# A two-layer hybrid block on one core: another order of TensorE in each step of the mixer, with what moves along with it

## The chip, the cores and the metric

The kernel runs on one core of a Trainium2 chip. The metric is device time in microseconds from start to end of one execution. TensorE does the matrix products (PE in the profile, PEld its weight loads), VectorE is DVE, ScalarE is ACT, GpSimd is POOL, and SyncE (SP) issues the transfers.

## The reference, cut to what matters

```python
for l in range(2):                      # x is 512 x 1024, float32
    h = rmsnorm(x, norm_mix[l])
    ua, cq, ckv, kr, qc, kc, vc, ud = split(h @ w_in[l])     # 15 column chunks of 128
    ya = conformer_conv(ua, ...)        # gate, 31-tap causal convolution, layernorm, silu, @ conv_pw
    yb = mla(cq, ckv, kr, ...)          # 4 heads, causal softmax attention over 512 keys
    yc = diff_attention(qc, kc, vc, positions, rel_bias, ...)   # 4 heads, 2 softmax maps each:
                                        # p = a0 - lam * a1, then rmsnorm of the result
    yd = multiscale_pool(ud, pool_w, pool_scale)   # windows of 2, 4, 8, 16 tokens
    x = x + concat(ya, yb, yc, yd) @ w_out[l]
    x = x + memory_cross_attention(rmsnorm(x), mem, ...)     # K and V from 256 memory tokens
    x = x + conv_glu_ffn(rmsnorm(x), ...)
return rmsnorm(x, norm_final)
```

## The kernel before

Activations lie transposed: 128 features per partition tile, 512 tokens in a row. A weight matrix is streamed in chunks of 128 output columns (1024x128 floats). Each chunk n goes through the same four stations, with two buffers per station (b = n % 2): SP loads it to `raw`, ACT rounds it to `wh` (`hi`, L695), an engine subtracts to get the rest `wl` (`lo` on DVE at L937, or `lower` on POOL at L650), and TensorE's `gemm` (L1247 to L1249) does 8 tiles of three products, wh x hi, wh x lo and wl x hi. The result in PSUM bank `G[n % 2]` is taken over by DVE (`scaled`, L962) or ACT (L845). `hi(n)` waits for the end of gemm n-2, and `gemm(n)` for `wl` of n.

In each layer 11 chunks of `w_in` come first, then the small products of the latents, and then the mixer: a loop over 38 steps t (`for t in range(STEPS)`, written out in Python for each engine, so the order on each queue is fixed). Steps 0 to 15 take one tile each of the MLA attention (one head, 128 queries, 512 keys), steps 16 to 31 one tile of differential attention with two maps. For a tile:

- TensorE computes the scores into `SC` (L1353, or two products at L1362), at the head of its step.
- DVE adds mask or bias, negates and takes the minimum (`negatives`, L1035). ACT does exp with the row sum (`exp_map`, L754).
- One step later DVE takes the reciprocal of the sum (L1054, L1060); for two maps it also makes a weight (L1062) and adds the second map to the first (L1064). POOL multiplies the tile by the reciprocal (L673).
- `TURN_LAG` = 3 steps later TensorE transposes the tile (`turn`, L1322) and ACT copies it to `ptr` (`evict_pt`, L769), after the `exp_map` of its own step.
- Every second step TensorE multiplies two transposed tiles with the values (`weighted_pair`, L1333); it waits for both copies. Pair n is at step 2n+5.

In the same steps lie one chunk gemm or none (`CHUNK_AT`: chunks 11 to 14 of `w_in` at steps 0 to 3, chunks 15 to 22 of the memory's keys at steps 5 to 12, chunks 23 to 30 of its values at 16, 18, 20, 22, 24, 27, 30, 33), the convolution's 62 taps on DVE (`convolve`), and small products that share the two PSUM banks `V`: transposed values `vc` (step 4), pooling `pool0/1` (8, 12), layernorm sums `ln_mean` (10) and `ln_var` (14), `pw0/1` of the convolution (22, 26), memory values `vx0..3` (20, 24, 28, 36), `sub0/1` for the norm of the differential result (29, 37). `V_USES` lists the uses of those banks in order, with the engine that frees each. At steps 34 to 37 the first two chunks of `w_out` begin.

In PE's step before the change: scores, turn, small products, weighted pair, chunk.

Of the kernel before, what the change touches and what calls it, by code (L numbers as in the profile page):

```python
# [27 lines left out]
P = 128  # L28
# [41 lines left out]
for _name, _w in (("ident", P), ("ones", P), ("bones", P), ("pair", P), ("invf", 1), ("phase", 1),  # L70
# [12 lines left out]
V_USES = ([("stat_mix", "dve"), ("stat_q", "dve"), ("stat_kv", "dve"), ("kr", "act"), ("uq0", "dve"),  # L83
           ("uq1", "dve"), ("uq2", "dve"), ("uq3", "dve")] + [(f"kn{h}", "act") for h in range(4)] +
          [("vm0", "act"), ("vm1", "act"), ("vc0", "act"), ("vc1", "act"), ("pool0", "dve"), ("ln_mean", "dve"),
           ("mla0", "dve"), ("pool1", "dve"), ("ln_var", "dve"), ("mla1", "dve"), ("vx0", "act"), ("pw0", "dve"),
           ("vx1", "act"), ("pw1", "dve"), ("diff0", "act"), ("vx2", "act"), ("sub0", "dve"), ("diff1", "act"),
           ("vx3", "act"), ("sub1", "dve"), ("stat_xa", "dve")] +
          [(f"xo{i}", "dve") for i in range(8)] + [("stat_ffn", "dve")])

Y_ORDER = {6: "pool0", 2: "mla0", 7: "pool1", 3: "mla1", 0: "pw0", 1: "pw1", 4: "diff0", 5: "diff1"}
# [12 lines left out]
V_FREED = {owner: [n for n, o in V_USES if o == owner] for owner in ("dve", "act")}  # L104

# [5 lines left out]
CHUNK_AT = {**{t: 11 + t for t in range(4)}, **{t: 10 + t for t in range(5, 13)},  # L111
            **{t: N_WV + i for i, t in enumerate((16, 18, 20, 22, 24, 27, 30, 33))}}

POOL_LO = {15: 25, 17: 26, 19: 27, 21: 28, 23: 29, 26: 30}
TURN_LAG = 3
STEPS = 38


def tile_at(u):

    return 2 * (u // 8) + u % 2, u // 2 % 4, u % 2

# [21 lines left out]
def block_program(nc, xT, memT, pos, const, vecs, small, w_first, w_main, w_up, w_down, w_last, out):  # L144
    with ExitStack() as ctx:
# [65 lines left out]
        memh, _ = sb("memh", [P, KT, M], F32R, a_at)  # L211
        meml, _ = sb("meml", [P, KT, M], F32R, a_at + 8192)
# [4 lines left out]
        psa, _ = sb("psa", [P, 528], F32, a_at + 24576)  # L217
        psb, _ = sb("psb", [P, 528], F32, a_at + 24576 + 2112)
# [62 lines left out]
        m_hi, m_lo = sem("mem_hi"), sem("mem_lo")  # L281
# [246 lines left out]
        with nc.Fori(0, L) as layer:  # L528
            with nc.Block() as block:
# [17 lines left out]
                def _(sp):  # L547
# [12 lines left out]
                    loads_of(2, 2, w_main, src_base=2)  # L560
                    sp.dma_start(sw[:], small[layer]).then_inc(sw_in, 16)
                    sp.dma_start(memf[:], mem_norm).then_inc(memf_in, 16)
                    loads_of(4, 12, w_main, src_base=4)
                    loads_of(16, 10, w_main, src_base=16)
# [14 lines left out]
                    for n in range(26, 35):  # L579
                        load(n, n % 2, w_main[layer, n])  # L580
                        if n == 26:
                            for u in (2, 3, 0, 1):
                                load_bias(u)
                        elif n < 31:
                            load_bias(2 * n - 50)
                            load_bias(2 * n - 49)
                        elif n == 31:
                            for u in (12, 13, 14):
                                load_bias(u)
                        elif n == 32:  # L590
                            load_bias(15)
# [15 lines left out]
                def _(pool):  # L607
# [6 lines left out]
                    def window_sums(i):  # L614

                        if i == 0:
                            pool.wait_ge(g_full, N_WK)
                        pool.wait_ge(g_dve, 14 + i)
# [47 lines left out]
                    for u in range(32):  # L666
                        if u < 16:
                            pool.wait_ge(rec_in, u + 1)
                            e, m = ering[:, u % RING, :], u
                        else:  # L670
                            pool.wait_ge(p_ready, u - 16 + 1)
                            e, m = dring[:, 2 * u % 8, :], 2 * u - 16
                        pool.tensor_scalar(e, e, rec[:, m:m + 1], None, ALU.mult).then_inc(scaled_in, 1)  # L673
                        if u in (3, 5):
                            window_sums(u // 2 - 1)
                        if u in (4, 6):
                            window_differences(u // 2 - 2)
                        if u in POOL_LO:
                            lower(POOL_LO[u])
# [8 lines left out]
                def _(act):  # L688
# [13 lines left out]
                    def v_freed(name):  # L702

                        act.wait_ge(v_dve, V_FREED["dve"].index(name) + 1)

# [20 lines left out]
                    for n in range(3, 11):  # L726
# [45 lines left out]
                    for t in range(STEPS):  # L772
# [7 lines left out]
                        if t == 4:  # L780
                            act.wait_ge(memf_in, 16)
                            act.wait_ge(g_full, N_WK)
                            for k in range(KT):
                                act.activation(memh[:, k, :], memf[:, k, :], ACT.Copy,
                                               scale=v("g_mem", k)).then_inc(m_hi, 1)
                            for i in range(2):
                                act.activation(vc[:, :, P * i:P * i + P],
                                               v_wait(f"vc{i}").rearrange("p (t f) -> p t f", t=4),
                                               ACT.Copy).then_inc(v_act, 1)
                        if t == 6:  # L790
                            act.wait_ge(lam_in, 2)
                            act.activation(lam[:, 2:4], lam[:, 0:2], ACT.Exp).then_inc(lam_e, 1)
# [3 lines left out]
                        if t in (8, 12):  # L796
                            i = t // 4 - 2
                            act.activation(b_hi[:, 6 + i, :], v_wait(f"pool{i}"), ACT.Copy,
                                           scale=v("pscale", i)).then_inc(y_hi, 1)
                        if t == 12:  # L800
                            for i in range(2):
                                if i == 0:
                                    act.wait_ge(cent, 1)
                                else:
                                    v_freed("ln_mean")
                                act.activation(sqx[:, i, :], acc[:, i, :], ACT.Square).then_inc(cent_sq, 1)
                        if t == 14:
# [7 lines left out]
                        if t in (22, 26):  # L815
                            i = (t - 22) // 4
# [8 lines left out]
                        if t in (20, 24, 28, 36):  # L825
                            g = {20: 0, 24: 1, 28: 2, 36: 3}[t]
                            act.activation(vx[:, :, GW * g:GW * g + GW],
                                           v_wait(f"vx{g}").rearrange("p (m f) -> p m f", m=2), ACT.Copy).then_inc(v_act, 1)
                        if t in (29, 37):
                            i = t // 8 - 3  # L830
                            act.activation(rtmp[:], v_wait(f"sub{i}"), ACT.Sqrt, bias=c("eps5"),
                                           scale=1.0 / 64).then_inc(root, 1)
                        if t in (34, 37):
# [96 lines left out]
                def _(dve):  # L930
# [18 lines left out]
                    def inverse(name, roots, cols=slice(0, S)):  # L949
# [4 lines left out]
                        if cols.stop == S:  # L954
                            ins.then_inc(v_dve, 1)
                            own_v(name)

                    def scaled(n, dst, b=None):
# [10 lines left out]
                              cq[:, 0, :], cq[:, 1, :], ckv[:], qk[:, 0, :], qk[:, 1, :], qk[:, 2, :], qk[:, 3, :],  # L969
                              vct[:, 0, :], vct[:, 1, :], ud[:, 0, PPAD:], ud[:, 1, PPAD:]]  # L970
# [16 lines left out]
                    def latents(part):  # L987
# [7 lines left out]
                        else:  # L995
                            dve.wait_ge(root, 3)
                            dve.reciprocal(sqx[:, 0, :], sqx[:, 0, :]).then_inc(v_dve, 1)
                            own_v("stat_kv")
# [4 lines left out]
                    for n in range(11):  # L1003
# [21 lines left out]
                        if n >= 3:  # L1025
                            convolve({8: 0, 9: 1, 10: 4}.get(n, 3))
# [11 lines left out]
                    for t in range(STEPS + 1):  # L1038
# [12 lines left out]
                        if 1 <= t < 17:  # L1051
                            m = t - 1
                            dve.wait_ge(e_done, m + 1)
                            dve.reciprocal(rec[:, m:m + 1], sums[:, m:m + 1]).then_inc(rec_in, 1)  # L1054
                        elif 17 <= t < 33:

                            u, k = t - 17, 2 * t - 18
                            dve.wait_ge(e_done, k + 2)
                            e0, e1 = dring[:, 2 * u % 8, :], dring[:, (2 * u + 1) % 8, :]
# [5 lines left out]
                        if t < 4:  # L1065
                            convolve(4)
                        elif t > 4:
                            convolve(3)
                        if t == 4:
# [5 lines left out]
                        if t in (9, 13):  # L1075
                            i = t // 4 - 2
# [3 lines left out]
                        if t == 11:  # L1080
# [7 lines left out]
                        if t in (12, 20):  # L1088
# [8 lines left out]
                        if 15 <= t < 19:  # L1097
                            inverse("ln_var", 4, slice(P * (t - 15), P * (t - 14)))
                        if t == 18:
# [547 lines left out]
```

## Time and profile before

| | us |
|---|---|
| median of 3 runs | 1760.46 (1758.02 to 1761.1) |
| the profiled execution, its own time | 1760.47 |
| its span, first to last instruction | 1758.6 |
| PE busy in the span | 1630.3 (93%) |
| DVE, ACT, POOL busy | 1108.6, 698.8, 308.2 |
| mean granted TensorE clock | 0.962 of 2.4 GHz |

Busy shares are means over stages of different kind. The mixer of layer 0 lies at 197 to 393 us, that of layer 1 at 1019 to 1214 us; the large matrix products fill most of the rest. A number in brackets at the end of a row is the idle time of the engine just before it, with what ended it.

### The profile page before, as it was taken

To read this page: it belongs to the slowest core of one execution; us is meant where nothing else is said; L and a number is where in the kernel's file an instruction comes from. 1 tells how busy PE (TensorE), PEld (TensorE's weight loads), DVE (VectorE), ACT (ScalarE), POOL (GpSimd) and SP (SyncE) were. 2 spreads that over 40 slices of the span, in tenths; PEclk is the share of its full clock that TensorE was granted. 3 is DMA by queue.
4 is the path that set the end of the run, shared out by engine and by line. 5 is a ranking of instruction groups with operands and counts; after the bars stand their busy time and mean duration, and the time that the engine had idled before them with its cause. 6 is when DMAs were issued, how large, how long until landed. Compare 5 with 4: busy or idle time off the path is not lost. (4 is left out here: it accounts for less than half of the span.)

```text
span 1758.6 us, 21905 instructions
## 1 busy us (share of the span) xinstructions
PE 1630.3 (93%) x7472; PEld 1253.1 (71%) x7472; DVE 1108.6 (63%) x1592; ACT 698.8 (40%) x1074; POOL 308.2 (18%) x216
## 2 busy tenths in 40 slices
PE   6889979889999999999998988898999999999996
PEld 3567566568767888888876666666877788888874
DVE  8967785655345764764764867665444675575576
ACT  3132345753244432432442243764343442342343
POOL 6510174522002000000020027551101100000002
PEclk9989899999999999999998998999999999999998
DMA  3242122313202232323324212322211222322323
GB/s 134 52 148 84 49 72 96 102 51 100 84 24 84 96 95 96 97 96 96 95 82 138 75 48 61 109 97 72 91 54 60 84 96 96 96 95 96 96 84 107
DMA packets 46206, 153.38 MB, mean 87 GB/s; under 512 B 5808, under 2 KB 6064, under 8 KB 45232
## 3 DMA queue, kind: packets, MB, share of 16 engines
q1 hardware_dynamic: 46128, 152.34, 26.8%
q8 instruction: 49, 0.80, 0.2%
q14 instruction: 29, 0.24, 0.0%
HBM read 144.97 MB, written 7.34 MB: 87 GB/s over the span
## 5 line engine op out<-in xcount | busy, mean ns | idle before, releaser
L695 ACT ACTIVATE wh<-raw 128x1024 fp32r<-128x1024 f32 x246 | 260.4, 1059 | 660.9 <-PE psum L1249 660.9
L1247 PE MATMUL psum<-a_hi,wh 128*128 128x512 f32 x1072 | 426.1, 397 | 7.9 <-DVE wl L937 7.5
L1249 PE MATMUL psum<-a_hi,wl 128*128 128x512 f32 x1072 | 420.0, 392 | 0.0
L1248 PE MATMUL psum<-a_lo,wh 128*128 128x512 f32 x1072 | 420.0, 392 | 0.0
L937 DVE TENSOR_TENSOR wl<-raw,wh 128x1024 fp32r<-128x1024 f32 x234 | 288.6, 1234 | 193.4 <-ACT wh L695 193.2
L1247 PE MATMUL psum<-b_hi,wh 128*128 128x512 f32 x608 | 240.8, 396 | 10.6 <-DVE wl L937 6.1
L1247 PEld LDWEIGHTS psum<-a_hi,wh 128*128 128x128 f32 x1072 | 203.0, 189 | 57.6 <-DVE wl L937 11.5
L1248 PE MATMUL psum<-b_lo,wh 128*128 128x512 f32 x608 | 237.4, 390 | 0.0
L1249 PE MATMUL psum<-b_hi,wl 128*128 128x512 f32 x608 | 237.4, 390 | 0.0
L1248 PEld LDWEIGHTS psum<-a_lo,wh 128*128 128x128 f32 x1072 | 203.2, 190 | 44.9 <-issue 2.9
L1249 PEld LDWEIGHTS psum<-a_hi,wl 128*128 128x128 f32 x1072 | 202.9, 189 | 42.5
L1135 DVE TENSOR_TENSOR x_sb<-x_sb,psum 128x512 f32<-128x512 f32 (+1 forms) x80 | 54.8, 685 | 168.9 <-PE psum L1249 168.9
L1247 PEld LDWEIGHTS psum<-b_hi,wh 128*128 128x128 f32 x608 | 114.5, 188 | 40.3 <-DVE wl L937 9.5
L1248 PEld LDWEIGHTS psum<-b_lo,wh 128*128 128x128 f32 x608 | 114.5, 188 | 24.2 <-issue 1.0
L1249 PEld LDWEIGHTS psum<-b_hi,wl 128*128 128x128 f32 x608 | 114.5, 188 | 24.0
L660 POOL COPY ssum<-sqx 128x512 f32<-128x512 f32 x6 | 3.7, 610 | 725.8 <-ACT sqx L712 725.8
L962 DVE TENSOR_TENSOR up<-psum,rbc 128x512 f32<-128x512 f32 x88 | 60.9, 692 | 87.1 <-PE psum L1249 87.0
L673 POOL TENSOR_SCALAR ering<-ering,rec 128x512 f32<-128x512 f32 x32 | 56.6, 1774 | 281.8 <-DVE rec L1054 281.2
L981 DVE SCALAR_TENSOR_TENSOR acc<-conv_in,vec,acc 128x512 f32<-128x512 f32 x120 | 100.2, 835 | 2.8
L663 POOL TENSOR_TENSOR ssum<-ssum,sqx 128x512 f32<-128x512 f32 x42 | 68.4, 1628 | 140.6 <-ACT sqx L712 140.6
L472 DVE TENSOR_SCALAR ind<-posf,cst 128x512 fp32r<-128x512 f32 x128 | 83.8, 723 | 1.0 <-PE psum L509 0.9
L1247 PE MATMUL psum<-memh,wh 128*128 128x256 f32 x256 | 82.5, 322 | 0.0
(214 smaller groups left out, 2188.3 us busy)
## 6 DMA issues: line engine op xcount, KB each, us to landing
raw<-in_w_main SPq DMA_DIRECT2D x106, 512.0 KB, 3.5
raw<-in_w_up SPq DMA_DIRECT2D x88, 512.0 KB, 3.5
raw<-in_w_down SPq DMA_DIRECT2D x32, 512.0 KB, 3.5
raw<-in_w_last SPq DMA_DIRECT2D x16, 384.0 KB, 2.9
bias_scratch<-stage SPq DMA_DIRECT2D x64, 64.0 KB, 1.6
bias<-bias_scratch SPq DMA_DIRECT2D x16, 256.0 KB, 3.9
raw<-in_w_first SPq DMA_DIRECT2D x6, 512.0 KB, 3.5
sw<-in_small SPq DMA_DIRECT2D x2, 1152.0 KB, 6.9
```

What stands on the lines that cost most here:

```text
L472: dve.tensor_scalar(ind[:, g % 4, :], posf[:, 0:S], c("turn"), posf[:, bass.ds(S + s * 8 + g, 1)], ALU.mult, ALU.is_le).then_inc(ind_in, 1)
L660: pool.tensor_copy(ssum[:], sqx[:, 0, :]).then_inc(ss_in, 1)
L663: pool.tensor_tensor(ssum[:], ssum[:], sqx[:, k % 2, :], ALU.add).then_inc(ss_in, 1)
L673: pool.tensor_scalar(e, e, rec[:, m:m + 1], None, ALU.mult).then_inc(scaled_in, 1)
L695: act.activation(wh[:, b].rearrange("p k m -> p (k m)")[:, 0:width], raw[:, b, 0:width], ACT.Copy).then_inc(w_hi, 1)
L937: dve.tensor_tensor(wl[:, b].rearrange("p k m -> p (k m)"), raw[:, b, :], wh[:, b].rearrange("p k m -> p (k m)").bitcast(F32), ALU.subtrac ...
L962: dve.tensor_tensor(dst, G[b], rbc[:], ALU.mult).then_inc(g_dve, 1)
L981: ins = dve.scalar_tensor_tensor(acc[:, i, :], win, w, acc[:, i, :], ALU.mult, ALU.add)
L1135: dve.tensor_tensor(x_sb[:, at, :], x_sb[:, at, :], G[b].rearrange("p (o s) -> p o s", o=1), ALU.add).then_inc(g_dve, 1)
L1247: pe.matmul(out_ap, wh[:, b, k, :], his[:, k, :], start=(begin and i == 0), stop=False)
L1248: pe.matmul(out_ap, wh[:, b, k, :], los[:, k, :], start=False, stop=False)
L1249: last = pe.matmul(out_ap, wl[:, b, k, :], his[:, k, :], start=False, stop=(end and i == len(tiles) - 1))
```

## The change

The order of TensorE in a step becomes turn, small products, weighted pair, scores, chunk. Along with it:

- One more chunk of `w_in` (12 in all) comes ahead of the mixer, and the order of these is changed, so that the pooling input `ud` is early (`IN_ORDER`). Chunks 12 to 30 now lie at steps 0 to 7, then 9, 11, ... 23, then 26, 29, 32.
- POOL no longer multiplies by the reciprocals; DVE does, with one more tensor_scalar of 128x512 per tile (it replaces L1062 in the two-map tiles). POOL makes `wl` of all chunks 15 to 32 instead of six, and does the pooling windows ahead of the mixer.
- The memory operands `memh` and `meml` are laid out so that each tile can be written as soon as chunk 14 has used the tile of `a_hi` in its place (`a_used`).
- `pool0/1` go to steps 1 and 3, `vc` to 6 and 8, `ln_mean` to 11, `ln_var` to 15, `vx0..3` to 18, 22, 28, 36, `pw0/1` to 23 and 25, `sub0` to 30. Every fourth pair (n % 4 == 0) is one step later.
- A bank that holds a sum for a square root is free after ACT has read it (`root`), not after DVE's reciprocal.

```diff
-CHUNK_AT = {**{t: 11 + t for t in range(4)}, **{t: 10 + t for t in range(5, 13)},
-            **{t: N_WV + i for i, t in enumerate((16, 18, 20, 22, 24, 27, 30, 33))}}
-POOL_LO = {15: 25, 17: 26, 19: 27, 21: 28, 23: 29, 26: 30}
+IN_ORDER = [0, 1, 2, 3, 4, 5, 6, 13, 14, 7, 8, 9, 10, 11, 12]
+CHUNK_AT = {t: 12 + i for i, t in enumerate((0, 1, 2, 3, 4, 5, 6, 7, 9, 11, 13, 15, 17, 19, 21, 23, 26, 29, 32))}
+VX_AT = {18: 0, 22: 1, 28: 2, 36: 3}
+POOL_LO = range(N_WK, N_OUT + 2)
+def pair_step(n):
+    return 2 * n + 5 + int(n % 4 == 0)
...
@@ gpsimd
-                    for u in range(32):
-                        if u < 16:
-                            pool.wait_ge(rec_in, u + 1)
-                            e, m = ering[:, u % RING, :], u
-                        else:
-                            pool.wait_ge(p_ready, u - 16 + 1)
-                            e, m = dring[:, 2 * u % 8, :], 2 * u - 16
-                        pool.tensor_scalar(e, e, rec[:, m:m + 1], None, ALU.mult).then_inc(scaled_in, 1)
...
+                    for i in range(2):
+                        window_sums(i)
+                        window_differences(i)
+                    for n in POOL_LO:
+                        lower(n)
@@ scalar
-                        if t == 19:
+                        if t == 21:
+                            act.wait_ge(cn, 2)
                             for i in range(2):
-                                act.wait_ge(cn, i + 1)
                                 act.activation(sqx[:, i, :], sqx[:, i, :], ACT.Silu, ...)
@@ vector
+                            dve.wait_ge(rec_in, m + 1)
+                            dve.tensor_scalar(e, e, rec[:, m:m + 1], None, ALU.mult).then_inc(scaled_in, 1)
                         elif 17 <= t < 33:
...
-                            step(dve.scalar_tensor_tensor(wgt[:, u:u + 1], rec[:, k + 1:k + 2], lam[:, 4:5],
-                                                          sums[:, k:k + 1], ALU.mult, ALU.mult))
-                            dve.scalar_tensor_tensor(e0, e1, wgt[:, u:u + 1], e0, ALU.mult, ALU.add).then_inc(p_ready, 1)
+                            step(dve.tensor_scalar(e1, e1, rec[:, k + 1:k + 2], lam[:, 4:5], ALU.mult, ALU.mult))
+                            dve.scalar_tensor_tensor(e0, e0, rec[:, k:k + 1], e1, ALU.mult,
+                                                     ALU.add).then_inc(scaled_in, 1)
@@ tensor
                     for t in range(STEPS):
+                        if TURN_LAG <= t < 32 + TURN_LAG:
+                            turn(t - TURN_LAG)
+                        if t in (1, 3):
+                            i = t // 2
+                            pe.wait_ge(ud_done, 2 * i + 2)
+                            product(f"pool{i}", ...)
...
+                        if t in VX_AT:
+                            g = VX_AT[t]
+                            pe.wait_ge(g_act, 8 + 2 * g + 2)
...
+                        if t in PAIR_AT:
+                            weighted_pair(PAIR_AT[t])
                         if t < 16:
                             h, qb, _ = tile_at(t)
                             bank_seen(t)
```

## Rows read from the trace of the kernel before

**Rows 1.** The page, part 1: busy us, share of the span, instructions, by engine.

```profile
PE 1630.3 (93%) x7472; PEld 1253.1 (71%) x7472; DVE 1108.6 (63%) x1592; ACT 698.8 (40%) x1074; POOL 308.2 (18%) x216
```

**Rows 2.** Stages: length, busy of PE, PEld, DVE, ACT, POOL, clock, DMA share, GB/s.

```profile
197.00:293.00 96.00, 83.09 (x488) 64.21 (x486) 67.55 (x112) 43.14 (x83) 48.02 (x33) 0.93 0.23 76
293.00:393.00 100.00, 87.12 (x574) 60.83 (x569) 62.80 (x136) 64.52 (x129) 42.57 (x25) 0.93 0.23 76
1116.00:1214.00 98.00, 85.34 (x568) 59.42 (x566) 62.41 (x136) 64.12 (x129) 42.17 (x25) 0.95 0.22 76
700.00:800.00 100.00, 99.57 (x440) 82.08 (x439) 67.39 (x91) 39.47 (x49) 0.00 (x0) 1.00 0.31 96
```

**Rows 3.** PE's timeline: start, length, instruction, count; heads of steps 0, 1, 16, 17.

```profile
196.62 1.02 PE L1353 MATMUL psum<-km,qm 128*128 128x512 f32 x2
202.93 1.02 PE L1353 MATMUL psum<-km,qm 128*128 128x512 f32 x2
...
293.18 1.13 PE L1362 MATMUL psum<-qk 32*128 32x512 f32 x4
...
297.69 1.13 PE L1362 MATMUL psum<-qk 32*128 32x512 f32 x4
...
300.36 1.13 PE L1362 MATMUL psum<-qk 32*128 32x512 f32 x4
```

**Rows 4.** PE's timeline, layer 0: waits in steps 5, 10, 21, 33 and after 37.

```profile
231.20 1.98 PE L1333 MATMUL psum<-ptr,vm 128*64 128x128 f32 x16 [5.18 <-ACT vc L787]
...
262.33 0.66 PE L1322 MATMUL psum<-cst,ering 128*128 128x128 f32 x4 [2.96 <-POOL ering L673]
...
265.97 3.78 PE L1276 MATMUL psum<-acc,cst 128*128 128x512 f32 x4 [2.98 <-DVE acc L981]
...
317.65 1.09 PE L1333 MATMUL psum<-ptr,vc 128*64 128x128 f32 x16 [2.21 <-DVE b_lo L1091]
...
367.75 1.11 PE L1322 MATMUL psum<-cst,dring 128*128 128x128 f32 x4 [3.50 <-POOL dring L673]
...
393.07 0.50 PE L1247 MATMUL psum<-b_hi,wh 128*128 128x512 f32 x1 [1.78 <-DVE wl L937]
```

**Rows 5.** A stretch with a lowered clock, columns as in rows 2.

```profile
262.00:272.00 10.00, 6.69 (x22) 4.39 (x23) 3.84 (x7) 1.29 (x3) 4.25 (x3) 0.66 0.15 52
```

**Rows 6.** Timeline of DVE and ACT in step 17, after the scores at 297.69.

```profile
298.96 0.69 DVE L1035 CUSTOM_DVE_ANT_0 dring<-psum,bias 128x512 f32<-128x512 f32 x1 [2.28 <-PE psum L1362]
...
299.69 0.72 ACT L754 ACTIVATE dring<-dring,mins 128x512 f32<-128x512 f32 x1 [0.51 <-DVE mins L1035]
...
301.12 0.57 ACT L769 ACTIVATE ptr<-psum 128x512 f32<-128x512 f32 x1
```

**Rows 7.** ACT's timeline in step 19: the silu between its table loads.

```profile
310.16 1.28 ACT L813 ACT_TABLE_LOAD   x1
311.46 1.52 ACT L813 ACTIVATE sqx<-sqx,vec 128x512 f32<-128x512 f32 x2
...
317.15 1.06 ACT L695 ACTIVATE wh<-raw 128x1024 fp32r<-128x1024 f32 x1
318.10 0.39 ACT L845 ACTIVATE vxt<-psum 128x256 f32<-128x256 f32 x1
```

**Rows 8.** Timeline of POOL and DVE around 318 us.

```profile
318.29 2.35 POOL L650 TENSOR_TENSOR wl<-raw,wh 128x1024 fp32r<-128x1024 f32 x1 [3.78 <-ACT wh L695]
318.83 1.83 DVE L1062 SCALAR_TENSOR_TENSOR wgt<-rec,lam,sums 128x1 f32<-128x1 f32 x1
```

**Rows 9.** Groups of DVE by form, 196 to 400 us: count, busy us, mean ns, idle before.

```profile
L981 DVE SCALAR_TENSOR_TENSOR acc<-conv_in,vec,acc 128x512 f32<-128x512 f32 x33 | 29.9, 906 | 0.8
L937 DVE TENSOR_TENSOR wl<-raw,wh 128x1024 fp32r<-128x1024 f32 x16 | 20.7, 1293 | 26.2 <-ACT wh L695 26.1
L1064 DVE SCALAR_TENSOR_TENSOR dring<-dring,wgt 128x512 f32<-128x512 f32 x16 | 12.0, 752 | 0.6
L953 DVE RECIPROCAL rtmp<-rtmp 128x128 f32<-128x128 f32 x8 | 7.4, 939 | 0.1
```

More of the change, by code:

```diff
@@ L79 @@
 SW_UQ0, SW_UQ1, SW_K, SW_V, SW_PW, SW_POOL, NSW = 0, 512, 1024, 1280, 1536, 2048, 2304
-V_USES = ([("stat_mix", "dve"), ("stat_q", "dve"), ("stat_kv", "dve"), ("kr", "act"), ("uq0", "dve"),
+V_USES = ([("stat_mix", "root"), ("stat_q", "root"), ("stat_kv", "root"), ("kr", "act"), ("uq0", "dve"),
            ("uq1", "dve"), ("uq2", "dve"), ("uq3", "dve")] + [(f"kn{h}", "act") for h in range(4)] +
[L85 to L91, printed above, removed]
+          [("vm0", "act"), ("vm1", "act"), ("pool0", "dve"), ("pool1", "dve"), ("vc0", "act"), ("vc1", "act"),
+           ("ln_mean", "dve"), ("mla0", "dve"), ("ln_var", "root"), ("vx0", "act"), ("mla1", "dve"), ("vx1", "act"),
+           ("pw0", "dve"), ("pw1", "dve"), ("diff0", "act"), ("vx2", "act"), ("sub0", "root"), ("diff1", "act"),
+           ("vx3", "act"), ("sub1", "root"), ("stat_xa", "root")] +
+          [(f"xo{i}", "dve") for i in range(8)] + [("stat_ffn", "root")])
+Y_ORDER = {6: "pool0", 7: "pool1", 2: "mla0", 3: "mla1", 0: "pw0", 1: "pw1", 4: "diff0", 5: "diff1"}
 Y_TILES = list(Y_ORDER)
@@ L209, in block_program @@
         vc, _ = sb("vc", [P, 4, GW], F32)
-        memh, _ = sb("memh", [P, KT, M], F32R, a_at)
-        meml, _ = sb("meml", [P, KT, M], F32R, a_at + 8192)
+        mems, _ = sb("mems", [P, KT, 2, M], F32R, a_at)
+        memh, meml = mems[:, :, 0, :], mems[:, :, 1, :]
         pt0, _ = sb("pt0", [P, 4, S], F32, a_at + 16384)
@@ L559, in _ @@
                     sp.dma_start(vec[:], vecs[layer]).then_inc(vec_in, 16)
-                    loads_of(2, 2, w_main, src_base=2)
+                    for n in (2, 3):
+                        load(n, n % 2, w_main[layer, n])
                     sp.dma_start(sw[:], small[layer]).then_inc(sw_in, 16)
                     sp.dma_start(memf[:], mem_norm).then_inc(memf_in, 16)
-                    loads_of(4, 12, w_main, src_base=4)
-                    loads_of(16, 10, w_main, src_base=16)
+                    for n in range(4, N_WK):
+                        load(n, n % 2, w_main[layer, IN_ORDER[n]])
+                    loads_of(N_WK, 10, w_main, src_base=N_WK)
                     def load_bias(u):
@@ L577, in load_bias @@
                         sp.dma_start(bias[u % 4], btab[head, qb]).then_inc(bias_in[u % 4], 16)
-                    for n in range(26, 35):
+                    for n in range(25, 35):
                         load(n, n % 2, w_main[layer, n])
[L581 to L591, printed above, removed]
+                        for u in BIAS_AFTER.get(n, ()):
+                            load_bias(u)
                     loads_of(35, N_UP - 35, w_main, src_base=35)
@@ L725, in _ @@
                         act.activation(sqx[:, i, :], sqx[:, i, :], ACT.Sigmoid).then_inc(gate_out, 1)
-                    for n in range(3, 11):
+                    for n in range(3, 12):
                         hi(n + 2)
@@ L954, in inverse @@
                         if cols.stop == S:
-                            ins.then_inc(v_dve, 1)
-                            own_v(name)
+                            step(ins)
                     def scaled(n, dst, b=None):
@@ L996, in latents @@
                             dve.wait_ge(root, 3)
-                            dve.reciprocal(sqx[:, 0, :], sqx[:, 0, :]).then_inc(v_dve, 1)
-                            own_v("stat_kv")
+                            step(dve.reciprocal(sqx[:, 0, :], sqx[:, 0, :]))
                             dve.scalar_tensor_tensor(ckv[:], ckv[:], v("kvn"), sqx[:, 0, :], ALU.mult,
@@ L1001, in latents @@
                             dve.tensor_tensor(cq[64:P, 1, :], cq[64:P, 1, :], rope[64:P, :], ALU.mult).then_inc(kr_in, 1)
-                    for n in range(11):
+                    for n in range(12):
                         if n == 0:
@@ L1234, in _, with gemm @@
                 def _(pe):
-                    def gemm(n, b, his, los, tokens=S, free=None, tiles=range(KT), ready=None, begin=True, end=True):
+                    def gemm(n, b, his, los, tokens=S, free=None, tiles=range(KT), ready=None, begin=True, end=True, used=None):
                         if begin:
@@ L1250, in gemm @@
                                              stop=(end and i == len(tiles) - 1))
+                            if used and i < len(tiles) - 1:
+                                last.then_inc(used, 1)
                         if end:
@@ L1268, in bank @@
                             before, owner = V_USES[V_AT[V_BEFORE[name]]]
-                            pe.wait_ge(v_dve if owner == "dve" else v_act, V_FREED[owner].index(before) + 1)
+                            freed = {"dve": v_dve, "act": v_act, "root": root}[owner]
+                            pe.wait_ge(freed, V_FREED[owner].index(before) + 1)
                         return V[V_BANK[name]]
@@ L1363, in _ @@
                                           start=True, stop=True).then_inc(s_full, 1)
-                        if TURN_LAG <= t < 32 + TURN_LAG:
-                            turn(t - TURN_LAG)
-                        if t == 4:
-                            pe.wait_ge(g_dve, 13)
-                            for i in range(2):
-                                ps = bank(f"vc{i}")
-                                for kb in range(4):
-                                    last = pe.transpose(ps[:, P * kb:P * kb + P], vct[:, i, kb * P:kb * P + P], ident)
-                                last.then_inc(v_full, 1)
@@ L1383, in _ @@
-                        if t in (20, 24, 28, 36):
-                            g = {20: 0, 24: 1, 28: 2, 36: 3}[t]
-                            pe.wait_ge(g_act, 8 + 2 * g + 2)
-                            ps = bank(f"vx{g}")
-                            for m in range(2):
-                                for k in range(2):
-                                    last = pe.transpose(ps[:, GW * m + P * k:GW * m + P * k + P],
-                                                        vxt[:, k, P * m:P * m + P], ident)
-                            last.then_inc(v_full, 1)
@@ L1402, in _ @@
-                        if t >= 5 and t % 2 == 1 and t <= 35:
-                            weighted_pair((t - 5) // 2)
                         n = CHUNK_AT.get(t)
```

175 lines of the change are left out of this document (89 added, 86 removed).

## The prediction

> **What bounds the kernel now.** I read the page's busy times first: PE is busy 93% of the span, the next engine 63% [rows 1]. Then stages: away from the mixer PE is busy 99.6 of 100 us at full clock, and nothing of the change reaches there; in the mixer it is busy 83 of 96 and 87 of 100 us, and the granted clock is 0.93 [rows 2]. So the change is worth what it does to PE's idle time and clock in two stretches of some 196 us. Last I read PE's timeline there, step by step.
>
> Prices of PE's work come from steps without a wait. Step 0 (a score and a chunk over 512 tokens) takes 202.93 - 196.62 = 6.31 us; 24 products at 0.227 are 5.45, so the score is 0.86. Step 16 takes 4.51 and step 17 takes 2.67 [rows 3]: two-map scores 1.06, turn 0.5, chunk over 256 tokens 2.95, weighted pair 1.03. The small products are multiples of the score's price: 0.86 for one input tile, 1.72 for two.
>
> With these, steps 0 to 15 hold 77.8 us of work (16 scores 13.8, 13 turns 6.5, pairs 0 to 5 6.2, four large and eight small chunks 45.4, small products 5.9) and take 293.18 - 196.62 = 96.6: **18.8 lost**. Of it 8.0 lie in step 5 and 8.8 in step 10. In step 5 pair 0 waits 5.18 for ACT, which is held by the copies of `memh` and `vc`; in step 10 a turn waits 2.96 for POOL, which was in its window sums, and `ln_mean` waits 2.98 for the last tap [rows 4]. What follows each is slower: the clock over 262 to 272 us is 0.66 [rows 5], so part of the time is at 1.2 GHz. From step 16 to 393.07 there are 99.9 us for 78.3 of work (two-map scores 17.0, 19 turns 9.5, ten pairs 10.3, eight small chunks 23.6, small products 7.0, 48 products of the first two output chunks 10.9): **21.6 lost**, 4.5 of it in the tail after step 37, the rest mostly in steps 19 to 22 and 32 and 33, where a turn waits 3.50 for POOL [rows 4]. Layer 1 repeats this (98 us in the last stretch [rows 2]).
>
> **Part by part: steps 0 to 15.** Chunk 11 goes ahead of the loop (5.45 earlier, same price; DVE's latents hold it up by about 1 us, and `qm` then comes 1 us sooner, net nothing) and chunk 23 comes in at step 15 (+2.95). The work is 77.8 - 5.45 + 2.95 = 75.3. The waits of step 5 and step 10 go: `vc` no longer shares a bank with pair 0, `memh` follows chunk 14 tile by tile, POOL does nothing a turn waits for, and the taps end at step 10 with `ln_mean` at 11. What is late next:
> - step 3: `pool1` needs the bank of `pool0`, which DVE frees only behind its eight `meml` pieces, the last of which ends 1.3 us after chunk 14, plus 0.75 for `b_lo`: 1.5 us.
> - step 9: after step 8 without a chunk, pair 2 waits for ACT's copy. From scores to that copy is the chain priced below, here with one map: 2.0 us.
> - step 11: DVE is now the fuller engine of steps 8 to 10. Its step is 0.7 `negatives` [rows 6], 0.16 reciprocal, the new tensor_scalar, three taps of up to 0.91 [rows 9]; for the tensor_scalar, which the trace of before does not show here, the bounds are 0.35 and the 0.75 of the 128x512 with two tensors [rows 9], and I take 0.55. It no longer has the 1.29 of `lo` [rows 9]. PE arrives about 2.5 us before the last tap.
> - POOL's subtraction of 2.35 us holds DVE: an operation that began at 318.83 ended at 320.66, just when POOL's from 318.29 was over [rows 8]. Eight of these fall in steps 3 to 10, mostly at a time when DVE waits for scores; I charge 1.3 us on the path, bounds 0 and 8 x 1.06 (2.35 less the 1.29 that DVE saves) = 8.5.
>
> Together 7.3 us instead of 18.8: **11.5 saved per layer.**
>
> **Part by part: steps 16 to the end.** The new order costs here. From the first score's start to the release of a pair is one chain: scores at 297.69, DVE at 298.96 (+1.27), exp at 299.69 (+2.0), the copy `ptr` at 301.12 after both exps (+3.43), done at +4.0, seen at about +4.2 [rows 3, 6]. Before, a chunk lay between the scores of an even step and the pair of the next, or the next scores did. Now an even step has no chunk and the scores come last, so between them and the pair lies only 1.06 of scores and 0.5 of turn: the pair waits 4.2 - 1.56 = 2.6 us. That holds for steps 17, 19 and 31: 7.8 us. Scores of the next step wait for DVE to have seen both maps (+2.6) in steps 21, 26, 28, 29: 3.6 us together.
>
> The small products are now directly behind what they need:
> - step 18: `vx0` needs chunk 24 copied out, ACT has `hi` 1.06 and the copy 0.39 first [rows 7]: 1.1 us beyond the turn.
> - step 22: `vx1` needs chunk 26 of step 21 copied out. ACT does this behind the silu of the same step, and the silu waits for nothing less than exp 21. DVE in step 20: two `negatives` 1.38, reciprocal 0.16, scaling 0.55 + 0.75, a quarter of the layernorm's reciprocal 0.94, and `cn` 2 x 0.69, priced as a `negatives`: 5.2 us [rows 6, 9], so its `negatives` 21 begin 5.5 us after scores 20 could be read. Counting from the end of chunk 26: exp 21 starts at +0.7, its pair and copy end at +2.7, table load 1.28, silu 1.52, `hi` 1.06, copy 0.39 [rows 7] end at +6.95. PE is there at +0.5: **6.5 us idle, and the clock falls**; at 0.66 over 10 us [rows 5] such a stretch costs 3.4, part of it hidden in waits; I take 2.3.
> - step 23: `pw0` needs the bank of `vx1`, copied behind exp 22: 2.7 us. Step 25: `pw1` needs the bank of `pw0`, which DVE frees behind the scaling of step 24 (1.27 + 1.38 + 1.5 + 0.75 after scores 24, against 1.56 on PE, and a hold by POOL of 0.4): 3.8 us.
> - the waits of step 32 and 33 go: with POOL out of the chain and a chunk at step 32 nothing is late there. The tail (sqrt, reciprocal, norm, split, then `wl` of chunk 33) is the same but for the longer look-ahead: 5.3 us against 4.5.
>
> Sum 7.8 + 3.6 + 1.1 + 6.5 + 2.3 + 2.7 + 3.8 + 5.3 = 33.1 instead of 21.6: **11.5 lost per layer**. It cancels the gain.
>
> What is left is the clock. Before, it fell four times a layer, behind waits of 2.2 to 5.2 us [rows 4, 5]. I have counted one fall after; waits of 2.5 to 3.8 in steps 11, 17 to 19, 25 and 31 are in the range in which it fell. With one or two of them, at 2.3 each, +3.5 us per layer, +7 in all. Elsewhere nothing: the chunks ahead of the loop and the stages after it keep their order, the bank release at ACT's root comes long before anything there wants the bank. The profiled execution before took 1760.47, as the median did, so the forecast is **1767.5 us**. Bounds of the unknown terms: clock 0 to 4 further falls a layer (-7 to +11 about the forecast), POOL's holds (-2.6 to +14), the tensor_scalar 0.2 either way in some 10 steps (4 each way).
>
> On POOL's holds the Trainium skill speaks against the change: Advanced Engine Details and Errata, GPSIMD Details, says that GpSimd shares a read and a write interface with VectorE and conflicts with its operations in a two-port mode or with two SBUF inputs. The trace agrees [rows 8]; by that rule each of the 18 subtractions could hold a tap or the new tensor_scalar for up to its whole length.
>
> **Rivals.**
> - *The stalls of steps 17 to 25 are shorter than I count* (chance 0.27, the faster side). One mechanism: if DVE reaches `negatives` 21 early, the silu runs under chunk 26 and vx1 waits only for `hi` and the copy, 1.0 instead of 6.5; then the clock stays and pw0 follows: 5.5 + 2.3 + 1 saved a layer on my count with no further falls. 1760.5 - 17.6 = **1743 us**. It decides if the silu ends ahead of chunk 26. For: ACT is busy only 64.5 of 100 us [rows 2]. Against: `cn` comes at the end of a 5.2 us DVE step, and ACT takes exp 21 before the silu.
> - *Gain and loss cancel and the clock adds nothing* (0.17): **1760 us**. Against: waits of 2.2 and more were followed by slow products in every such case of rows 4.
> - *POOL's subtractions hold DVE through the taps* (0.13, slower): bound 8.5 instead of 1.3 a layer, and more at step 25 and 20. 1767.5 + 14 = **1782 us**. It decides if a POOL subtraction begins while taps run; then a step of DVE is 3.9 + 2.35, above PE's 4.3 to 5.3. Against: each begins just behind the end of a chunk, when DVE is waiting or at `negatives`, which reads PSUM.
> - The change could fail to do what it says only in the first half, if `ln_mean` still waited for taps; that is inside the range.
>
> **How the numbers follow.** Forecast 0.43, the rivals 0.27, 0.17 and 0.13. A measurement of this kernel tells 0.2% (3.5 us) from no change, so same is 1757 to 1764. The first rival is the faster side, 0.27. Same is the cancelling case, 0.17. The forecast's own range, 1764 to 1775, and the POOL case are slower, 0.56. For 8 in 10 the range reaches over half of the faster case and over the POOL case: 1746 to 1783.
>
> **What would show it.** Right: PE waits of about 6 us ahead of L1389's successor (`vx1`) on ACT in each layer, waits of about 2.6 us ahead of weighted pairs on ACT, no wait of 5 us in step 5, no PE wait on POOL; the first half of the mixer about 11 us shorter for equal work and the second about 11 longer. Wrong: a second half no longer than 100 us, or DVE without idle time in steps 3 to 10 with PE waiting at every pair.

## The result, and the profile after

Before 1760.59 us (median of 4 runs, 1758.02 to 1761.10), after **1787.06 us** (4 runs, 1784.64 to 1792.57): ratio 1.0158, 95% interval 1.0132 to 1.0183, slower by 26.5 us. The forecast said slower, but by 7, and the time lies above its range. The profiled execution took 1784.64 us, 24.2 more than the one of before.

Stages of the changed kernel, columns as in [rows 2]: layer 0 from step 0 to the head of step 16, step 16 to the second output chunk, two stretches inside, and the second half in layer 1.

```profile
201.00:285.60 84.60, 75.84 (x489) 59.05 (x488) 63.76 (x110) 41.96 (x82) 24.71 (x10) 1.00 0.24 82
285.60:404.00 118.40, 90.43 (x546) 61.61 (x545) 62.33 (x135) 65.70 (x128) 19.31 (x9) 0.87 0.19 63
300.17:312.30 12.13, 9.79 (x49) 7.72 (x50) 7.10 (x16) 4.48 (x11) 0.38 (x1) 0.58 0.25 86
320.17:349.40 29.23, 16.81 (x88) 10.39 (x88) 11.53 (x28) 15.39 (x30) 4.71 (x2) 0.77 0.16 55
1118.43:1236.82 118.39, 90.46 (x547) 61.69 (x545) 62.30 (x135) 65.70 (x128) 19.32 (x9) 0.87 0.19 63
```

The first half has lost its stalls and runs at full clock. The second takes 118.4 us in either layer, in layer 0 where it took 99.9, at 0.87 instead of 0.93 [rows 2]; 41 us of it are at 0.58 and 0.77. Step 16 starts at 285.65 and not at 293.18; the second output chunk goes on at 404.03 and not at 393.07 [rows 4]; in layer 1 at 1236.82 and not at 1214.07. So layer 0 loses 11.0 us and layer 1 11.8, together 22.8 of the 24.2.

PE's timeline in the second half of layer 0, its longer waits:

```profile
290.24 1.09 PE L1326 MATMUL psum<-ptr,vm 128*64 128x128 f32 x16 [2.34 <-ACT ptr L758]
303.09 1.98 PE L1326 MATMUL psum<-ptr,vm 128*64 128x128 f32 x16 [2.34 <-ACT ptr L758]
326.08 1.11 PE L1368 MATMUL psum<-cst,vxt 128*128 128x128 f32 x4 [5.91 <-ACT vxt L835]
333.88 2.90 PE L1268 MATMUL psum<-sqx,sw 128*128 128x512 f32 x3 [2.95 <-ACT vx L817]
349.43 2.41 PE L1268 MATMUL psum<-sqx,sw 128*128 128x512 f32 x3 [3.60 <-DVE b_lo L1096]
378.47 1.09 PE L1326 MATMUL psum<-ptr,vc 128*64 128x128 f32 x16 [2.37 <-ACT ptr L758]
404.03 0.51 PE L1236 MATMUL psum<-b_hi,wh 128*128 128x512 f32 x1 [1.77 <-DVE wl L927]
```

All but the last, which was there before, are where the forecast put them: pairs at steps 17, 19 and 31, vx1, pw0, pw1. The same instruction, a pair of sixteen, takes 1.09 us at 290.24 and 1.98 at 303.09: the second runs at 1.2 GHz, the granted clock from there to 312.30 is 0.50. ACT's timeline in steps 21 and 22 shows what PE waits for (reads of the row sums left out):

```profile
321.41 0.57 ACT L758 ACTIVATE ptr<-psum 128x512 f32<-128x512 f32 x1
322.00 1.28 ACT L803 ACT_TABLE_LOAD   x1
323.29 1.52 ACT L803 ACTIVATE sqx<-sqx,vec 128x512 f32<-128x512 f32 x2
324.72 1.04 ACT L688 ACTIVATE wh<-raw 128x1024 fp32r<-128x1024 f32 x1
325.66 0.36 ACT L835 ACTIVATE vxt<-psum 128x256 f32<-128x256 f32 x1
326.04 1.28 ACT L743 ACT_TABLE_LOAD   x1
331.25 0.72 ACT L743 ACTIVATE dring<-dring,mins 128x512 f32<-128x512 f32 x1 [3.92 <-DVE mins L1023]
331.97 0.70 ACT L743 ACTIVATE dring<-dring,mins 128x512 f32<-128x512 f32 x1
332.68 0.57 ACT L758 ACTIVATE ptr<-psum 128x512 f32<-128x512 f32 x1
333.15 0.58 ACT L817 ACTIVATE vx<-psum 128x512 f32<-128x512 f32 x1
```

The silu (L803) stands ahead of the weight copy and `vxt`. Then, behind the table load for exp, ACT idles 3.92 us until DVE has seen the scores of step 22, and `vx`, which needs nothing of these scores, stands behind their exponentials and gets done at 333.7; PE, which wanted it, goes on at 333.88.

### The profile page after: what moved, and what is told of

It reads as the page before. It is cut to its first block and busy times, and to the rows that moved or that the text cites. A ratio compares the mean times of both kernels' runs of the same rounds, so it can differ in the third digit from the quotient of the medians.

```text
span 1782.9 us, 21837 instructions
## 1 busy us (share of the span) xinstructions
PE 1626.5 (91%) x7472; PEld 1253.0 (70%) x7472; DVE 1118.2 (63%) x1600; ACT 700.5 (39%) x1074; POOL 261.3 (15%) x176
## 5 line engine op out<-in xcount | busy, mean ns | idle before, releaser
L1236 PE MATMUL psum<-a_hi,wh 128*128 128x512 f32 x1072 | 426.1, 397 | 12.3 <-DVE wl L927 11.9
L927 DVE TENSOR_TENSOR wl<-raw,wh 128x1024 fp32r<-128x1024 f32 x210 | 261.5, 1246 | 141.2 <-ACT wh L688 141.2
L652 POOL TENSOR_TENSOR wl<-raw,wh 128x1024 fp32r<-128x1024 f32 x36 | 87.9, 2440 | 326.5 <-ACT wh L688 326.5
L1237 PEld LDWEIGHTS psum<-b_lo,wh 128*128 128x128 f32 x608 | 115.0, 189 | 24.2 <-issue 1.0
L1238 PEld LDWEIGHTS psum<-b_hi,wl 128*128 128x128 f32 x608 | 114.7, 189 | 24.4
L1236 PE MATMUL psum<-mems,wh 128*128 128x256 f32 x256 | 84.4, 330 | 0.0
```

The source lines that it names most:

```text
L652: pool.tensor_tensor(wl[:, n % 2].rearrange("p k m -> p (k m)"), raw[:, n % 2, :], wh[:, n % 2].rearrange("p k m -> p (k m)").bitcast(F32) ...
L927: dve.tensor_tensor(wl[:, b].rearrange("p k m -> p (k m)"), raw[:, b, :], wh[:, b].rearrange("p k m -> p (k m)").bitcast(F32), ALU.subtrac ...
L1236: pe.matmul(out_ap, wh[:, b, k, :], his[:, k, :], start=(begin and i == 0), stop=False)
L1237: pe.matmul(out_ap, wh[:, b, k, :], los[:, k, :], start=False, stop=False)
L1238: last = pe.matmul(out_ap, wl[:, b, k, :], his[:, k, :], start=False, stop=(end and i == len(tiles) - 1))
```

## The experiments

e1, e2, e3 and e7 are the changed kernel with one edit, e5, e6 and e8 to e11 with two or more, and e4 is the kernel before with one. Each is compared with the kernel before on the same chip; that took 1762.1 us for e1 to e4, 1760.1 for e5 to e8 and 1759.6 for e9 to e11, so differences between these groups are good to about 2 us. "First" and "last" say where a step's scores stand in PE's order. Half times are of layer 0, second half (step 16 to the second output chunk).

| kernel | median us | to before, 95% | second half us | its clock |
|---|---|---|---|---|
| before (first) | 1760.6 | 1 | 99.9 | 0.93 |
| after (last) | 1787.1 | 1.0132 to 1.0183 | 118.4 | 0.87 |
| e1, e5, e6, e8 (first) | 1738.8, 1738.2, 1737.6, 1736.8 | 0.984 to 0.989 | 97.5 (e1) | 0.93 |
| e2 silu late (last) | 1783.3 | 1.0100 to 1.0135 | 117.0 | 0.85 |
| e3 filled (last) | 1772.5 | 1.0043 to 1.0076 | 108.3 | 0.98 |
| e4 before, last from step 16 | 1804.2 | 1.0222 to 1.0256 | 120.6 | 0.84 |
| e7, e11 side work first (last) | 1750.9, 1747.8 | 0.993 to 0.997, 0.992 to 0.995 | 100.8 (e7) | 0.93 |
| e9, e10 side work first (first) | 1726.0, 1721.3 | 0.980 to 0.984, 0.976 to 0.980 | 88.3 (e10) | 1.00 |

**e1: the order alone, undone.**

```diff
 for t in range(STEPS):
+    [the score block of step t]
     turn(t - TURN_LAG); small products; weighted pair
-    [the score block of step t]
     chunk
```

> The changed kernel with one part undone: TensorE issues the scores at the head of each step again, ahead of turn, small products and weighted pair; placement of chunks and products, POOL's and DVE's work stay changed. Theory (waits of the second half come from scores last, with chunk-free even steps): the wait ahead of the pairs of steps 17, 19, 31 falls from 2.34 to about 1.0 us, the one on pw1 from 3.6 to about 1.1, that on pw0 from 2.95 to about 1, that on vx1 stays above 5 us; about 9 us a layer, and some 3 to 6 us a layer of slow clock with it: 1787 - 28 = about 1759 us, 1753 to 1766. Rival (the order is nearly without effect, the placement of chunks and small products makes the loss): 1780 us or more.

Measured 1738.83 (1737.30 to 1740.99), better than any theory had it. So the new order costs 48 us, and the rest of the change gains 22. The stages of its layer 0, and the longest wait left:

```profile
200.36:283.90 83.54, 77.45 (x489) 59.23 (x487) 65.14 (x110) 41.61 (x82) 25.09 (x10) 0.98 0.26 83
283.90:381.44 97.54, 83.67 (x546) 56.43 (x545) 66.30 (x135) 65.77 (x128) 19.02 (x9) 0.93 0.23 76
314.54 1.11 PE L1382 MATMUL psum<-cst,vxt 128*128 128x128 f32 x4 [3.76 <-ACT vxt L835]
```

The first half is only 1 us shorter than after's: the order costs in the second half, 97.5 us here against 118.4.

**e2: silu behind the copies of step 21.**

```diff
-    if t == 21: silu
     ...
     hi(n + 2); copy of chunk to vxt
+    if t == 21: silu
```

> The changed kernel with ACT's silu of step 21 moved behind the chunk's hi and copy in the same step, nothing else. Theory: vx1 at step 22 waits about 1.3 us instead of 5.9, pw0 at step 23 0.6 us more than its 2.95; 3.9 us a layer and one fall of the clock less, 1 to 5 us a layer: 1768 to 1777 us, most likely 1773. Rival (ACT is late in these steps whatever its order, the wait moves on to pw0 in full): within 2 us of 1787.

Measured 1783.34 (1779.73 to 1784.49): a smaller gain than expected, between the two ranges. The wait for `vxt` fell from 5.91 to 3.12, but the one for pw0 stayed at 2.49 and that product still runs slow:

```profile
322.54 0.66 PE L1368 MATMUL psum<-cst,vxt 128*128 128x128 f32 x4 [3.12 <-ACT vxt L830]
330.26 3.71 PE L1268 MATMUL psum<-sqx,sw 128*128 128x512 f32 x4 [2.49 <-ACT vx L812]
```

The waits of this half are 3.6 us fewer, but the half is only 1.4 us shorter (117.0 against 118.4), at a clock of 0.85 instead of 0.87: more of its work is slow.

**e3: waits filled.** Unread products of `wh` and `mems` into a free bank, ahead of the waits of steps 17, 19, 22, 23, 25 and 31; they add work and take no wait away.

```diff
     turn(t - TURN_LAG)
+    if t in WARM: [WARM[t] unread products into the chunk's next bank]
```

> The changed kernel with extra products on TensorE that nothing reads: weights of the next chunk against the memory operand, 512 columns each, into the product bank that the next chunk overwrites; 9 at steps 17, 19 and 31, 24 at 22, 12 at 23, 14 at 25, which at 0.227 us each is a little less than the wait that stands there. Theory (the forecast missed the clock: some 11.8 us a layer are work at 1.2 GHz, on top of 24.5 us of waits): the clock stays at 1.00 in steps 16 to 31 and the time falls by 16 to 23 us, to 1764 to 1771. Rival 1 (slow work only fills time in which TensorE would wait anyway): 1787 within 4 us. Rival 2 (fillers come out longer than the waits): longer than 1787.

Measured 1772.53 (1764.89 to 1773.12), 14.5 us faster than without these products and just above the expected range. The profiled execution is the fastest of the four, 7.6 us below the next. Its second half:

```profile
286.20:394.50 108.30, 97.86 (x624) 69.26 (x622) 62.47 (x135) 65.77 (x128) 19.44 (x9) 0.98 0.22 69
327.24 1.95 PE L1268 MATMUL psum<-sqx,sw 128*128 128x512 f32 x4 [0.20 <-ACT vx L817]
```

77 products more and 10 us less, in layer 1 as well (108.3 us): the clock is 0.98, and pw0 takes 1.95 where it took 3.75. So in this execution 10 us of each layer's loss in the changed kernel were work at the lower clock, and not waiting; by the medians it is 7.

**e4: the order alone, on the kernel before, from step 16.** The score block behind the weighted pair, nothing else.

> The kernel before with the changed order of TensorE alone, from step 16 on (turn, small products, pair, then scores, chunk); steps 0 to 15, the placement of all work and the engines' shares stay as before. Theory (the order costs only where no chunk lies between the scores of an even step and the pair of the next, here steps 26 and 28): 3 to 7 us a layer with the clock, 1767 to 1775 us. Rival (the order by itself is the whole loss): 1785 us. Rival (no effect): 1760 us.

Measured 1804.15 (1800.79 to 1804.90), +42 us: above the theory and both rivals. The second half of layer 0, and two of its waits:

```profile
289.11:409.70 120.59, 96.12 (x570) 67.01 (x568) 58.26 (x136) 64.56 (x129) 42.45 (x25) 0.84 0.19 62
315.01 1.76 PE L1333 MATMUL psum<-ptr,vc 128*64 128x128 f32 x14 [4.24 <-DVE b_lo L1091]
364.85 2.05 PE L1276 MATMUL psum<-sqx,cst 128*128 128x512 f32 x2 [3.92 <-ACT vx L827]
```

Step 16 begins at 289.11 here, so this half is 20.7 us longer than before (120.6 against 99.9); that of layer 1 is 22.6 longer (120.9 against 98.3). The waits in this stretch sum to 24.4 us (before: 12.9), 11.5 more; the other 9 go with the clock, 0.84 instead of 0.93. So the order costs this much without the new chunk places too, on which my theory had made it depend, and most of the added waiting is for side work (`b_lo`, `vx`), not for the copies `ptr`.

**e5, e6, e8: what is left with scores first.** e5 moves the silu as e2 does. e6 adds fillers to it (steps 9, 11, 22, 25). e8 gives `wl` of chunks 17 to 22 back to DVE in e1.

> Scores at the head of each step again, and ACT's silu of step 21 behind the chunk's hi and copy; all else as in the changed kernel. With scores last the later silu brought 4 us in all, since the wait moved on to pw0. Theory (with scores first ACT has exp 22 behind it early, so that the wait of 3.76 us ahead of vx1 goes and nothing takes its place, and the 3.3 us of slow work after it go too): 4 to 7 us a layer below the run with scores first alone (1738.8), 1725 to 1731 us. Rival (the wait moves on again): 1735 to 1739.

> The same with products that nothing reads in four places where TensorE waited: 10 at step 9, 11 at step 11, 5 at 22, 4 at 25 (0.227 us each, next chunk's weights against the memory operand, into the bank the next chunk overwrites). Theory (part of what is left is the clock, here the slow ln_mean of step 11 and pw1 of step 25): 2 to 4 us a layer below the same kernel without them, 1720 to 1726 us. Rival (they only shift work): equal within 2 us, or above it where a filler is longer than its wait.

> Scores first as in the first run of that name (1738.8 us), and the subtractions for chunks 17 to 22 on DVE instead of POOL (steps 3 to 9). Rival of the forecast under test (POOL's subtractions hold DVE through the taps for more than they save): DVE gains 2.35 of hold for 1.23 of work each, the waits ahead of pair 2 and ln_mean shrink, 1730 to 1735 us. Theory (most of each POOL subtraction falls where DVE waits, a hold of some 0.6 us each; six times 1.23 - 0.6 is added ahead of ln_mean): 2 to 4 us a layer more, 1743 to 1747 us.

Measured 1738.15, 1737.56 and 1736.76; none differs from e1 by more than runs and chips scatter. In e5 and e6 the rival held, e8 lies between its two ranges. In e5 the wait only moved, from `vxt` to pw0, which still runs slow (two of its products take 2.04 us, in e3 all four took 1.95):

```profile
319.28 2.04 PE L1268 MATMUL psum<-sqx,sw 128*128 128x512 f32 x2 [3.40 <-ACT vx L812]
```

In e8 the first halves of the two layers took 80.4 and 81.9 us where e1's took 83.6 and 84.1: with six subtractions on DVE that stage is 2 to 3 us shorter, yet the whole kernel by only 2.1, against a kernel before that was 2.1 faster on that chip. So there is little to gain from moving these six.

**e7: side work first, scores last.** From step 16 ACT does the copies `ptr` and `vx` and the evictions of pw ahead of the step's exponentials, DVE pw's `b_lo` ahead of `negatives`. PE's order stays.

```diff
 # ACT, step t >= 16
-    exp_map(2 * t - 16); exp_map(2 * t - 15)
     evict_pt(t - TURN_LAG)
+    vx (t in 18, 22); pw (t in 23, 25)
+    exp_map(2 * t - 16); exp_map(2 * t - 15)
 # DVE
+    pw's b_lo (t in 24, 26)
     negatives(...)
```

> The changed kernel with TensorE's order as changed (scores last); from step 16 on ACT does the copy of the transposed tile, vx0/1 and pw0/1 ahead of the step's exps, and DVE the rest of pw0/1 ahead of the step's negatives. Theory (scores last costs because ACT and DVE begin each step with what waits for the scores, and all else of the step stands behind it, while TensorE now asks for that ahead of its own scores): the waits of 2.34 us at the pairs of 17, 19, 31, of 2.95 on pw0 and 3.6 on pw1 go, 13.6 us a layer, vx1 keeps its 5.9; with 5 to 8 us a layer of clock 1745 to 1755 us. Rival (the chain over scores, negatives and exp itself has become too long, whatever the order on ACT and DVE): 1778 us or more.

Measured 1750.91 (1749.30 to 1752.59), as expected: 36 of the 48 us come back without touching PE's order. The four waits on pairs 17 and 19, pw0 and pw1 are gone, the pair of step 31 waits 1.34 instead of 2.37, and `vx0` at step 18 now waits 2.81 instead of 1.04 for its `vxt`. ACT's timeline in step 22, to be set beside that of after:

```profile
321.77 0.60 ACT L768 ACTIVATE vx<-psum 128x512 f32<-128x512 f32 x1 [0.72 <-PE psum L1372]
325.69 0.72 ACT L743 ACTIVATE dring<-dring,mins 128x512 f32<-128x512 f32 x1 [2.03 <-DVE mins L1027]
```

`vx` is done 3.3 us before the exponentials it stood behind. The wait for `vxt` (5.46 us) is left, since that copy still stands behind them.

**e9, e10, e11: side work first with scores first, and with the silu late.** e9 has scores first, silu late, and `vx`, pw and `b_lo` first; e10 has `ptr` first too; e11 is e7 with the silu late.

> Scores at the head of the step as before, the rest as changed, SiLU behind the weight copy of step 21, and on ScalarE the copies of vx0, vx1 and the evictions of pw0, pw1 ahead of the step's exponentials, on VectorE pw's b_lo ahead of the negatives. With the scores at the head the negatives and exponentials are no longer late, so the theory (side work waits behind score work that itself waits for TensorE) expects little left to gain: 1733 to 1738 us, against 1738.2 without the side work first. A rival (side work first is worth its own durations whatever the order of TensorE) expects about half of the 36 us that it gave with the scores last: 1718 to 1726 us.

> As the kernel before this one, and the copy of the transposed probabilities too ahead of the exponentials from step 16 on. It holds the exponentials back by a copy of about 0.7 us a step where they are ready: the theory expects 1732 to 1742 us, the rival 1715 to 1726 us.

> The changed order of TensorE (scores last), side work first on ScalarE and VectorE from step 16, and SiLU behind the weight copy and the copy of vxt at step 21. With side work first 1750.9 was measured, with a wait of 5.46 us for vxt left in layer 0; SiLU late took 2.8 us of that wait away and gave a pw wait of 2.5 back. The theory expects 1746 to 1752 us; a rival, that the long wait also costs the slow clock behind it, expects 1738 to 1744 us.

Measured 1725.96 (1723.84 to 1729.71), **1721.29** (1718.63 to 1723.11) and 1747.82 (1746.27 to 1748.31). e11 is as expected. For e9 and e10 my theory was too narrow and the rival held: moving side work ahead of the two exponentials is worth 17 us with scores first too (e5 to e10), and 36 with scores last (e2 to e11). e10 beats the kernel before by 2.2% (ratio 0.9764 to 0.9803) and the changed one by 66 us. Its layer 0, ACT around step 21, and PE's pw0:

```profile
202.25:286.59 84.34, 78.92 (x489) 61.03 (x487) 65.48 (x110) 41.73 (x82) 24.73 (x10) 0.96 0.25 82
286.59:374.86 88.27, 78.60 (x546) 53.97 (x545) 66.51 (x135) 66.04 (x128) 19.06 (x9) 1.00 0.25 84
314.94 1.52 ACT L839 ACTIVATE sqx<-sqx,vec 128x512 f32<-128x512 f32 x2
316.37 0.57 ACT L758 ACTIVATE ptr<-psum 128x512 f32<-128x512 f32 x1
316.84 0.58 ACT L768 ACTIVATE vx<-psum 128x512 f32<-128x512 f32 x1
318.73 0.72 ACT L743 ACTIVATE dring<-dring,mins 128x512 f32<-128x512 f32 x1
317.57 1.95 PE L1272 MATMUL psum<-sqx,sw 128*128 128x512 f32 x4 [0.56 <-ACT vx L768]
```

pw0's wait is 0.56, no wait in that half but the tail's two is over 1.2 us, and the clock is 1.00: the second half takes 88.3 us for 75.4 of work. Between e10 and e11 lie 26.5 us, with side work first in both: this is what scores last costs when only the `vxt` copies still stand behind the exponentials. That this copy is the reason is read from the waits for `vxt` (2.81 and 2.63 us in e11, 0.25 and 0.44 in e10) and wasn't tried.

## Why the prediction was wrong in size

**Right: the first half.** The stalls of steps 5 and 10 are gone. Steps 0 to 15 take 84.7 us, 9.4 of them lost; the forecast had 82.6 and 7.3. Chunk 11 ahead of the loop moved step 0 by 4.35 us (200.97 against 196.62 [rows 3]). PE's waits in these steps sum to 8.7 us; two of them weren't in the forecast, 0.51 at step 6 for `b_lo` and 1.27 at step 13 for `ptr`. Seven of DVE's fifteen tensor_scalars of these steps took 1.58 to 2.27 us, each at the time of a subtraction on POOL; how much of the excess that is, isn't shown. POOL and DVE around 230 us, and the form's group over 201 to 286:

```profile
228.92 2.41 POOL L652 TENSOR_TENSOR wl<-raw,wh 128x1024 fp32r<-128x1024 f32 x1 [4.01 <-ACT wh L688]
229.94 1.67 DVE L1045 TENSOR_SCALAR ering<-ering,rec 128x512 f32<-128x512 f32 x1
231.53 4.51 DVE L970 SCALAR_TENSOR_TENSOR acc<-conv_in,vec,acc 128x512 f32<-128x512 f32 x3
L1045 DVE TENSOR_SCALAR ering<-ering,rec 128x512 f32<-128x512 f32 x15 | 16.0, 1066 | 0.5
```

Undisturbed this tensor_scalar takes 0.49; the mean is 1.07 where I took 0.55, and here it ends just behind POOL's, at 231.6 and 231.3. `ln_mean` waited 2.84 us for the last tap, as forecast (2.5).

**Right: the waits of the second half.** I had 7.8 + 3.6 + 1.1 + 6.5 + 2.7 + 3.8 = 25.5 us; they sum to 24.6 (thirteen waits: the six above ahead of the tail, and seven of 0.3 to 1.3). The chain from scores to `ptr`, the silu's place and the bank hand-offs were read rightly from the rows of before.

**The step that failed: the clock.** "I have counted one fall after; ... With one or two of them, at 2.3 each, +3.5 us per layer." From step 16 to 404.03 are 118.4 us for 75.35 of work, 43.0 lost: 24.6 of waits, 4.5 in the tail as before the change (5.3 forecast), and 13.9 left, against 2.3 in the sum and 3.5 added behind it. Counted row by row against the forecast's prices, five stretches run slow: scores and chunk of step 17, +1.5; pair, scores and chunk from 303.09 to 312.29, +4.2; vx1 with its pair and scores, +1.5; pw0 with its pair and scores, +2.9; pw1 with its pair, +1.8; together 11.9. The other 2.0 are rows a little above their price. The first of the five lies right behind the pair at 290.24, which itself ran at full speed:

```profile
290.24:297.00 6.76, 6.76 (x46) 5.47 (x47) 3.55 (x8) 5.22 (x8) 0.00 (x0) 0.75 0.35 119
291.26 1.48 PE L1395 MATMUL psum<-qk 32*128 32x512 f32 x4
```

A product of the chunk at either level:

```profile
307.38 0.42 PE L1237 MATMUL psum<-mems,wh 128*128 128x256 f32 x1
316.82 0.28 PE L1237 MATMUL psum<-mems,wh 128*128 128x256 f32 x1
```

They start 0.22 and 0.12 us after each other. I listed waits of 2.5 to 3.8 in steps 11, 17 to 19, 25 and 31 as "in the range in which it fell" and then charged one or two of them beside the fall at vx1, 5.8 us in all, where five stretches came: at steps 17, 19, 22, 23 and 25. That is the upper bound I had named (four further falls, +11), not the term. Their mean of 2.4 us is the price I had taken (2.3): it was the count that failed. e3 confirms the term by removing most of it: clock 0.98, 14.5 us less by the medians in spite of 77 products more per layer. With 11.9 in place of 5.8 the forecast would have been 6.1 us a layer higher, 1779.7. What is left to the profiled execution (1784.6) is 2.4 a layer: 2.1 more in the first half, the 2.0 of small excesses, 0.9 less of waits and 0.8 less of tail.

**Also wrong: what the order is worth.** The prediction set the order's loss against the gain of the same change as two sums that cancel. e1 shows 22 us of gain and 48 of loss. Scores first would have been 22 us better than before, and a long wait does not act alone: in e2 one was halved and 4 us came back, in e5 it moved on; in e7 four went together, and the clock went from 0.87 to 0.93 and 36 us came back.

**The rivals.** Shorter stalls (1743): vx1 waited 5.91 against 6.5 forecast, so no. Cancelling (1760): failed for the clock, as the sentence against it said. POOL's holds (1782): real, but the first half lost only 2.1 us a layer more than forecast, and e8 finds 2 to 3 us there in undoing six of them; most of the distance to 1787 is the clock.

## What to carry to other kernels

In these runs `vx` waited on ACT behind exponentials of which it needs nothing (331.25 to 333.15 in after), since each engine's queue has a fixed order. Before moving an instruction ahead on the busiest engine, look where the work that releases it stands on its own engine's queue, and move that ahead too. Here the same side work ahead of the exponentials was worth 36 us with the new order and 17 with the old. Where a stretch has several waits of 2 to 4 us, charge slow work behind each, not only behind the longest: of the six waits over 2 us ahead of the tail, five had it. Unread products in the waits can tell how much of a loss is the clock; read the clock and the medians of several executions with it.

## What the runs showed of the hardware

Waits of the same length had different effects. Behind the 2.34 us that ended at 290.24 the pair ran at full speed, the scores after it took 1.42 us instead of 1.06 and the chunk 4.13 instead of 2.98; behind the 2.34 us that ended at 303.09, with one of 1.04 shortly before, all the work to 312.29 was slow, 4.2 us of it in excess; behind the 2.37 us that ended at 378.47 nothing was, the clock to 382 is 1.00. A single wait's length didn't decide it in these rows. With the same order of PE, e3's unread products kept the clock of this half at 0.98. Filling waits cannot be carried over blindly: in e6, with fewer and shorter waits, filling them gained nothing (1737.56 against 1738.15).
